# Output projection moved into the block of the head groups, with half of its outputs begun in the last pair

## What is computed

```python
ya = _dilated_attention(heads_a(qa), heads_a(ka), heads_a(va))       # 8 heads
yb = _neighbourhood_attention(heads_b(qb), heads_b(kb), heads_b(vb), rpb)  # 8 heads
fn(u) = jnp.concatenate([ya, yb], axis=-1) @ w_out
z = DEEPNORM_ALPHA * h + resid_w * gate * fn(u)
h = _layer_norm(z) * ln_g[layer, j] + ln_b[layer, j]
```

## Time and profile before

| | us |
|---|---|
| median of 3 runs | 1906.39 |
| lowest, highest | 1903.69, 1907.27 |
| the profiled execution | 1901.04 |
| its span, in which all times below are counted | 1899.3 |

### The profile page before, as it was taken

One profiled execution on the slowest core, in us unless ns is written; L12 is line 12 of the kernel. 1 busy time (PEld: TensorE's weight loads), 2 busy tenths in 40 slices (PEclk: granted clock), 3 DMA queues, 4 the chain that ended last, 5 costly groups with the idle time before them and its releaser, 6 DMA issues. The chain is left out here.

```text
span 1899.3 us, 27248 instructions
## 1 busy us (share of the span) xinstructions
PE 1842.8 (97%) x10006; PEld 1483.7 (78%) x10006; DVE 1186.0 (62%) x1921; ACT 805.3 (42%) x1416; POOL 582.5 (31%) x393
## 2 busy tenths in 40 slices
PE   5999999999999999999999988999999999999997
PEld 3788888887888878777777766878888888888886
DVE  5876676665687883443454555888444444467888
ACT  4533333333345473543454554275333333333543
POOL 0263344432991000000023420015444344359400
PEclk9999999999999999999999999999999999999999
DMA  9265655554975333332235436222242324288733
GB/s 341 59 222 174 192 169 195 182 187 155 335 273 176 111 128 102 124 93 65 76 86 102 86 121 218 101 92 89 90 132 84 111 89 133 73 284 285 237 102 122
DMA packets 180539, 284.81 MB, mean 150 GB/s; under 512 B 14548, under 2 KB 95032, under 8 KB 180280
## 3 DMA queue, kind: packets, MB, share of 16 engines
q1 hardware_dynamic: 170784, 252.69, 41.1%
q10 hardware_dynamic: 9624, 30.39, 5.1%
HBM read 220.91 MB, written 62.12 MB: 149 GB/s over the span
## 5 line engine op out<-in xcount | busy, mean ns | idle before, releaser
L1591 PE MATMUL f_ps<-f_uh,f_ops 128*128 128x512 f32 x2496 | 776.3, 391 | 6.7 <-DVE f_ul L1396 1.9
L1591 PEld LDWEIGHTS f_ps<-f_uh,f_ops 128*128 128x128 f32 x2496 | 469.2, 188 | 111.3 <-issue 10.8
L1591 PE MATMUL f_ps<-f_ul,f_ops 128*128 128x512 f32 x1248 | 486.2, 390 | 0.0
L1591 PEld LDWEIGHTS f_ps<-f_ul,f_ops 128*128 128x128 f32 x1248 | 234.7, 188 | 48.0
L934 POOL TENSOR_TENSOR f_sums<-f_raw 128x512 f32<-128x512 f32 x80 | 111.6, 1395 | 519.4 <-DMA f_raw<-in_ffn_w_gate 231.5
L1444 DVE TENSOR_TENSOR f_dl<-f_blocks,f_dh 128x1024 fp32r<-128x1024 f32 (+1 forms) x146 | 210.2, 1456 | 66.7 <-ACT f_dh L1153 66.5
L1153 ACT CAST f_dh<-f_blocks 128x1024 fp32r<-128x1024 f32 (+1 forms) x146 | 144.2, 990 | 216.0 <-PE f_ps L1724 209.3
L1265 DVE TENSOR_TENSOR f_ops<-f_sums,f_ops 128x512 fp32r<-128x512 f32 x160 | 126.5, 791 | 120.7 <-ACT f_ops L999 120.6
L2156 POOL TENSOR_TENSOR x_b_bias<-x_b_runs,x_b_mask 128x384 f32<-128x384 f32 x48 | 52.3, 1120 | 467.6 <-DMA x_b_runs<-bias_table 415.0
L1724 PE MATMUL f_ps<-f_dh 128*128 128x512 f32 x496 | 193.1, 389 | 0.7 <-DVE f_ev L1481 0.7
L1724 PE MATMUL f_ps<-f_dl,f_dh 128*128 128x512 f32 x496 | 193.0, 389 | 0.0
(11 more groups left out here) (316 smaller groups left out, 3053.7 us busy)
## 6 DMA issues: line engine op xcount, KB each, us to landing
f_hidden<-acc SPq DMA_DIRECT2D x154, 256.0 KB, 4.1
f_blocks<-f_hidden SPq DMA_DIRECT2D x154, 256.0 KB, 3.3
f_blocks<-in_ffn_w_down SPq DMA_DIRECT2D x132, 256.0 KB, 5.5
f_raw<-in_ffn_w_gate SPq DMA_DIRECT2D x20, 1024.0 KB, 6.2
f_raw<-in_ffn_w_up SPq DMA_DIRECT2D x20, 1024.0 KB, 6.9
f_aw<-in_w_ada ACTq DMA_DIRECT2D x28, 512.0 KB, 4.1
acc<-in_w_ada ACTq DMA_DIRECT2D x28, 512.0 KB, 3.8
acc<-in_x SPq DMA_DIRECT2D x16, 512.0 KB, 5.5
```

Source lines behind the costliest of these rows:

```text
L1591: done = nc.tensor.matmul(ps[:, bank, :], l[:, k, :], r[:, k, :], start=fresh and k == 0 and m == 0, stop=closed and k == HK - 1 and m == ...
```

## The change

The output projection's block and ProjectionAhead are gone; all of it is now at the end of mixer_phase, with no barrier between.

- Steps 115 to 130 of the loop have 6 matmuls each between score and turn (out_begin): k = 0 to 3 for the eight outputs j = 2 to 7, 0 and 1, two outputs at a time in the two banks of in_pj. When two outputs of j = 2 to 7 are through k = 3, ScalarE copies them to SBUF (move, into o_part1 to o_part3), and the next two begin in the same banks. Outputs 0 and 1 stay in their banks.
- After the loop TensorE does the rest in the order of the code at the end of the diff. VectorE adds the three kept parts to the residual before the tail.
- GpSimd now scales all of w_out by the gate row: k = 0 to 2 ahead of the biases of the last pair, k = 3 to 7 behind them. ScalarE casts w0, w1, w2, w3 in steps 104, 106, 114, 116 and the mixed rows 0, 1, 2, 3 and 6 in steps 113 to 117; VectorE subtracts one step later. The rest of the splits stand behind the loop.
- The mixed rows of pairs 6 and 7 are split straight from y, and not stored and loaded; those of 0 to 5 are loaded into ut_lo, once the last projection is done.
- h is loaded as eight DMAs, four when the last x_o product is done, four when the last mixed row is split; then the rows of ln_g and ln_b.

```diff
+    MIXED = (0, 1, 2, 3, 6, 4, 5, 7)
+    EARLY_J = (2, 3, 4, 5, 6, 7, 0, 1)
+    OUT_FIRST = LAST + 3
+    OUT_SLOTS = U + LAG - OUT_FIRST
+    OUT_K = HP
+    HIGH_W, HIGH_Y = {LAST - 8: 0, LAST - 6: 1, LAST + 2: 2, LAST + 4: 3}, {1: 0, 2: 1, 3: 2, 4: 3, 5: 6}
+    y_raw = ut_lo[:, :, :].bitcast(F32)
...
+    def out_range(s):
+        total = 3 * OUT_K * len(EARLY_J)
+        x = s - OUT_FIRST
+        return (total * x // OUT_SLOTS, total * (x + 1) // OUT_SLOTS) if 0 <= x < OUT_SLOTS else (0, 0)
...
+            def load_weights(k):
+                sp.dma_start(out_mem.raw[k][:, :], w_out[P * k:P * k + P, :]).then_inc(ow_ld[k], 16)
+
+            def load_mixed(k):
+                sp.dma_start(y_raw[:, k, :], y_t[k]).then_inc(oy_ld[k], 16)
...
                     sp.wait_ge(y_st, 16 * HP)
-                    ahead.load_mixed(sp)
+                    for k in range(HP):
+                        load_mixed(k)
...
+                if p == NP - 2:
+                    sp.wait_ge(q_lo, NP)
+                    load_weights(0)
+                    sp.dma_start(out_mem.gates[:, :], out_gate.broadcast_to([P, D])).then_inc(gate_ld, 16)
+                    load_weights(1)
+                    sp.wait_ge(exped, UA)
+                    load_weights(2)
                 if p == NP - 1:
-                    ahead.load_third(sp)
+                    sp.wait_ge(y_st, 16 * (NP - 2))
+                    for k in (4, 5):
+                        load_mixed(k)
+                    load_weights(4)
+                    sp.wait_ge(b_ready, 2 * RBS * 3 * HP)
+                    load_weights(5)
+                    sp.wait_ge(low, LAST + UN)
+                    load_weights(6)
+                    load_weights(7)
...
-            store(NP - 1)
+            sp.wait_ge(pv, HALVES * NP)
+            for t in range(TT):
+                if t == 4:
+                    sp.wait_ge(oy_lo, KT)
+                sp.dma_start(acc[:, t, :], h_t[P * t:P * t + P, :]).then_inc(h_ld, 16)
+            sp.wait_ge(scaled, KT)
+            for i, r in enumerate((lng, lnb)):
+                sp.dma_start(out_mem.rows[:, i, :], r.broadcast_to([P, D])).then_inc(bc_ld, 16)
+            sp.wait_ge(parted, 3)
+            rows.load(sp)
+            for t in range(TT - 1):
+                tail.store(sp, t)
...
+            def scale(k):
+                pool.wait_ge(ow_ld[k], 16)
+                nc.gpsimd.tensor_tensor(out_mem.raw[k][:, :], out_mem.raw[k][:, :], out_mem.gates[:, :],
+                                        ALU.mult).then_inc(scaled, 1)
+
             for p in range(HP, NP):
+                if p == NP - 1:
+                    pool.wait_ge(gate_ld, 16)
+                    for k in range(3):
+                        scale(k)
                 pool.wait_ge(r_ld, 16 * QR * (p - HP + 1))
...
+            for k in range(3, KT):
+                scale(k)
...
+            def high_weights(k):
+                act.wait_ge(scaled, k + 1)
+                if k == 2:
+                    act.wait_ge(pj_mm, len(JOBS))
+                if k == 4:
+                    act.wait_ge(b_ready, 2 * RBS * 3 * HP)
+                nc.scalar.copy(out_mem.wh[k][:, :], out_mem.raw[k][:, :]).then_inc(ow_hi, 1)
+
+            def high_mixed(k):
+                if k < NP - 2:
+                    act.wait_ge(oy_ld[k], 16)
+                    of = y_raw[:, k, :]
+                else:
+                    if k == NP - 2:
+                        act.wait_ge(pj_mm, len(JOBS))
+                    act.wait_ge(y_out, HALVES * (k + 1))
+                    of = y
+                nc.scalar.copy(ut_hi[:, k, :], of).then_inc(oy_hi, 1)
...
+            def move(n):
+
+                j = EARLY_J[n]
+                act.wait_ge(begun, n + 1)
+                if n == 0:
+                    act.wait_ge(qk, LAST)
+                nc.scalar.copy(out_mem.parts[j // 2][:, NB * (j % 2):NB * (j % 2) + NB], pj[:, j % 2, :]).then_inc(moved, 1)
...
+                for j in moved_in(s - 1):
+                    move(EARLY_J.index(j))
...
+                if s in HIGH_W:
+                    high_weights(HIGH_W[s])
+                if p == NP - 1 and m in HIGH_Y:
+                    high_mixed(HIGH_Y[m])
...
+            for s in range(U + LAG, U + LAG + 1):
+                for j in moved_in(s - 1):
+                    move(EARLY_J.index(j))
+            for k in (4, 5):
+                high_weights(k)
+                high_mixed(k)
+            high_weights(6)
+            high_mixed(7)
+            high_weights(7)
...
+                if s - 1 in HIGH_W:
+                    low_weights(HIGH_W[s - 1])
+                if p == NP - 1 and m - 1 in HIGH_Y:
+                    low_mixed(HIGH_Y[m - 1])
...
+            for k in (4, 5):
+                low_weights(k)
+                low_mixed(k)
+            low_weights(6)
+            low_mixed(7)
+            low_weights(7)
+            came.set_eps(dve)
+            dve.wait_ge(h_ld, 16 * TT)
+            dve.wait_ge(moved, 6)
+            for t in (1, 2, 3):
+                nc.vector.scalar_tensor_tensor(acc[:, t, :], acc[:, t, :], ALPHA, out_mem.parts[t][:, :], ALU.mult, ALU.add
+                                               ).then_inc(parted, 1)
+            dve.wait_ge(parted, 3)
+            dve.wait_ge(bc_ld, 32)
...
+            def out_ready(k):
+                pe.wait_ge(ow_lo, k + 1)
+                pe.wait_ge(oy_lo, mixed_done(k))
+
+            def out_begin(s):
+
+                for x in range(*out_range(s)):
+                    j, k, part = out_at(x)
+                    n = EARLY_J.index(j)
+                    if part == 0:
+                        if n < 2:
+                            out_ready(k)
+                        if n < 2 and k == 0:
+                            wait_taken(pe, len(JOBS) - 2 + n)
+                        elif k == 0:
+                            pe.wait_ge(moved, n - 1)
+                    done = out_product(j, k, part, pj[:, j % 2, :], k == 0, k == OUT_K - 1 and j >= 2)
+                    if k == OUT_K - 1 and part == 2 and j >= 2:
+                        done.then_inc(begun, 1)
+
+            def out_part(j, to, first, last):
+
+                for k in range(first, last):
+                    if j < 2 or first == 0:
+                        out_ready(k)
+                    for part in range(3):
+                        done = out_product(j, k, part, to, k == 0 or (2 <= j < 8 and k == OUT_K), k == KT - 1)
+                if last == KT:
+                    done.then_inc(mm, 1)
...
             for s in range(U + LAG + 1):
                 p, m = s // NU, s % NU
-                if s < U and s != seam + 1:
+                if s < U:
                     score(s)
-                if s in (seam + 1, seam + 2):
-                    if s == seam + 1:
-                        wait_taken(pe, len(JOBS) - 1)
-                    ahead.product(pe, s - seam - 1)
+                out_begin(s)
                 if LAG <= s < U + LAG:
                     turn(s - LAG)
                 if p + 1 < NP:
                     fill(p, m)
-                if s == seam:
-                    score(s + 1)
                 if half_due(s) is not None:
                     multiply(half_due(s))
+            pe.wait_ge(low, U)
+            for j in (8, 9):
+                out_part(j, sc[:, j % 2, :], 0, OUT_K)
+            pe.wait_ge(p_out, U)
+            for j in (10, 11):
+                out_part(j, tr[:, j % 2, :], 0, OUT_K)
+            for j in (0, 1):
+                out_part(j, pj[:, j, :], OUT_K, KT)
+            pe.wait_ge(y_out, HALVES * NP)
+            for j in (2, 3):
+                out_part(j, o[:, j % 2, :], OUT_K, KT)
+            for j in (4, 5):
+                pe.wait_ge(summed, j - 3)
+                out_part(j, pj[:, j % 2, :], OUT_K, KT)
+            for j in (6, 7):
+                pe.wait_ge(summed, j - 3)
+                out_part(j, o[:, j % 2, :], OUT_K, KT)
+            for j in (8, 9):
+                out_part(j, sc[:, j % 2, :], OUT_K, KT)
+            for j in (10, 11):
+                out_part(j, tr[:, j % 2, :], OUT_K, KT)
+            for j in (12, 13):
+                pe.wait_ge(summed, j - 7)
+                out_part(j, pj[:, j % 2, :], 0, KT)
+            for j in (14, 15):
+                pe.wait_ge(summed, j - 7)
+                out_part(j, o[:, j % 2, :], 0, KT)
```

More of the change, by code:

```diff
@@ L2711, in __init__ @@
+        self.gates = m.at("o_gates", [P, D], 34 * BL)
         self.rows = m.at("o_rows", [P, 2, D], 34 * BL)
[L2712 to L2714 removed]
+        self.parts = [None if kb is None else m.at(f"o_part{t}", [P, D], 1024 * kb) for t, kb in enumerate(self.PARTS)]
```

309 lines of the change are left out of this document (90 added, 219 removed).

## The result

The kernel after the change took 1911.17 us (median of 15 runs, 1907.53 to 1915.99), the kernel before 1903.70 us in its 15 runs (1900.72 to 1907.27). The ratio is 1.0034, with a 95% interval of 1.0026 to 1.0042: some 6.5 us slower (7.5 us by the medians). The profiled executions span 1908.3 and 1899.3 us, 9.0 apart.

The account below looks back on a forecast made before the run. It took the end of the last pair, the landing of h and VectorE's 50.2 us tail as what matters. 18.7 - 23.4 + 4.9 + 2.6 = +2.8 us gave 1909.2 us on a before-median of 1906.39, range 1899 to 1916.

Parts of the forecast that it names:

- Part 3: Pair before the last: w0's cast at step 104 waits for the scaled row, so TensorE stops 4.9 us.
- rival (c): Last pair: GpSimd's scalings of w4 to w7 hold up VectorE's divides; +8.3 us, 1914.7; chance 0.22.
- Part 4: Slow TensorE clock: 1.7 us behind the new gap, 0.9 around steps 112 to 115; +2.6 us.
- Part 1: Last pair, from step 112 to the last x_o: 90 new matmuls and new waits make it 18.7 us longer.
- Part 2: Last x_o to the end: no block boundary or memory trip, so VectorE's tail starts earlier; 23.4 us shorter.
- Rival (a): Pair before the last: the gates are in time, its wait and clock charge go; -3.8 us, 1902.6; chance 0.12.
- Rival (b): Last pair runs at earlier pairs' pace with no waits but the first; -4.1 us, 1902.3; chance 0.10.

Follow-up runs that it names:

- late casts: Kernel after, with ScalarE's casts of w0 and w1 moved from steps 104 and 106 to 108 and 110: 1905.55 us, ratio to before 1.0006.
- early gate row: Kernel after, with the gate row, w0 and w1 issued ahead of the 16 value loads of pair 6: 1904.52 us, ratio to before 1.0003.
- additional matmuls: Kernel with the three edits and scalings in four pieces, plus 12 unused matmuls at the start of step 115: 1893.99 us, ratio to before 0.9945.
- last-row-first kernel: Kernel after, with the last mixed row split second instead of sixth behind the loop: 1909.23 us, ratio to before 1.0025.
- staggered outputs: Kernel after, with paired outputs one behind the other instead of by turns, from the second pair on: 1908.34 us, ratio to before 1.0018.
- all edits together: Kernel after with the three edits and scalings in pieces: 0.9954; with additional matmuls 0.9945; with first output matmul one step later instead 0.9940.
- the three edits: Kernel after with early gate row, staggered outputs and last row first: 1898.63 us, ratio 0.9967; with scalings in four pieces too, 1895.88 us.

## Why the prediction was right, and which terms were off

It forecast 1909.2 us in a range of 1899 to 1916, with 0.42 on slower and 0.43 on no difference. The time, 1911.17, lies in the range, 2.0 us above the forecast; its ratio to before is above the bound of 0.2%, so the outcome is "slower", the one with 0.42 and by a hair not the likeliest. That the time came so near was in part luck. The forecast stood on the median of three runs of before, 1906.39; over 15 runs it is 1903.70, 2.7 us less, and this error covers part of the other. As a difference to before, +2.8 us were forecast and 6.5 measured (7.5 by the medians, 9.0 between the two profiled executions). The path was right: the wait, its place and its cause, the last pair's length and the gain behind it. The terms below that were sized too small put the ratio above the bound. Step by step:

- **Part 3, the new wait (right, 2.4 us short).** Found in the earlier trace rows alone, it is shown by two edits (late casts, early gate row) that take it away and get back 5.3 and 5.9 us. Seen from the common starting point, the cast's start and end hit to 0.1 us. The term that was mis-sized is "Queued behind the subtraction (to 1102.4) on VectorE: minimum 106 and divide 104. Turn 104 on TensorE needs that divide (1103.4)": subtraction and divide were priced as if GpSimd stood still, though the same paragraph had GpSimd scale w0 and the diff has it go on to w1 and w2. They took 1.1 and 1.5 us longer. The rival (c) had that very mechanism, with a row for it; it was put into the last pair, where it costs nothing, and not in the pair before, where it sat on the critical chain.
- **Part 4, the clock (mis-sized, about 1 us short).** 2.1 us in place of 1.7 behind the stop, and 1.4 in place of 0.9 behind step 115's wait, measured against the trace with additional matmuls, in which the clock stays up. The kernels of the edits paid 1.6 to 2.8 us for this second fall, so the kernel after, in its trace, was at the cheap end.
- **Part 1, the last pair (18.7 forecast).** Start of step 115's matmuls 6.7 (forecast 6.6); waits of 0.39 and 1.52 at steps 117 and 118 (0.5 and 1.6), 1.65, 1.65 and 1.73 for the copies (1.85, 1.8, 1.15), 0.57 at the last x_o (0.5). The sum is nearly exact, and yet the last pair took 1.3 us more than that. A bracket shows less than a stop costs: consecutive matmuls overlap, the turn at 1144.14 is 0.49 long and the next matmul would have started 0.25 behind it, so the stop of 1.65 costs 1.89. Over the six stops of the last pair this makes 1.2 us.
- **Part 2, behind the last x_o (right).** 0.6 us later start, 1.3 us shorter tail, for the reason given with the profile. The sum took "1.3 us for each 512 KB" from a row that gives 15.8 / 10 = 1.6 as it stands (4 MB behind 1 MB); h was there 1.1 us later than the sum had it, and the three additions took 3.5 us in place of 3.9, so that little of it is left at the start of the tail.
- **Not in the sum:** 1.4 us ahead of the changed code in this one execution, and 0.7 us between the tail and the second FFN. The first is no part of the change. The second is there in the profile of the last-row-first kernel too (1247.19 to 1248.92, 1.7 us); which instruction of the block's end it is was not tried and stays open.

Rival (a) did not come true: the gates were not in time. The kernel in which they are takes 0.03% more than before, where this rival had 3.8 us less; 1904.52 is near its 1902.6 only because both of the prediction's times stand on the high median of three runs. Rival (b) did not either, since all the waits of part 1 stand where they were forecast; staggered outputs take two of them away. So the idle time of the last pair can be used, for 0.5 to 0.6% with all edits together. In the kernel after, a cast queued 5 us ahead of its data, the copies out of the two banks, the stops beside GpSimd and a load behind the last split used the gain up.

## What to carry to other kernels

When work is moved into an earlier step of an in-order queue, look up when its input lands before anything else: here the price was the distance from the queue's place to the landing, what stood behind it in the queues, and the slow clock, and issuing the gate row and two rows of w_out ahead of the value loads took it away. Where GpSimd and VectorE both work from SBUF on a critical chain, try shorter GpSimd instructions for the same work; here that took away the stops that moving work had left. Behind an idle stretch of TensorE count the slow clock too (1.4 to 2.8 us behind 3.05 us of waiting): work that is ready, put ahead of the waiting matmuls, won 2.7 us here, and matmuls that nobody reads won 1.7.

## What was not expected of the hardware

- The same GpSimd work in four short instructions takes a third longer (10.60 for 7.95 us in the pair before the last, 11.54 for 9.75 in the last) and still makes the program faster (with the three edits by 2.5 us).
- A divide held up for 2 us beside GpSimd cost nothing in the last pair, where divides run ahead of their turns, and went through in full in the pair before, where the look-ahead had been used up.
- How long the clock stays down behind a like stop differs between executions of like code. After step 115's wait of 3.05 us the stretch 1132 to 1134 had a mean of 0.93 in the kernel after (matmuls from 1129.39), while in the kernel with the last row first (matmuls from 1128.07) it was still at 0.59. To the next score it is 5.98 and 7.24 us: 1.3 us of difference that no edit explains.
- Whether the clock falls at all differs too. The kernel before had stops of 1.42 and 0.61 us ahead of the first x_o of its last pair and kept 1.00 (x_o 2.84 us); the kernel that starts the output matmuls one step later had 1.42 and 0.75 us at the same place and fell (x_o 4.50 us). What decides it, no run here shows.
